# Which engine adds the residual: GpSimd for all tiles but one, VectorE keeps products and low parts

## The chip, the cores and the metric

One core of a Trainium2 chip runs the whole program. Its engines are TensorE (matrix products), VectorE, ScalarE, GpSimd and SyncE (which here only issues DMAs); they run their own instruction streams and meet at semaphores. The metric is the device time of one execution in microseconds.

## What is computed

The reference is one inference step of a decoder trunk with two layers, for 256 prompt tokens and 8 x 4 sample tokens, so 288 tokens of width 1024 in all. Layer 0 mixes tokens by dilated and sliding-window attention, layer 1 by retention; each is followed by a squared-ReLU MLP. Every one of these four sublayers stands between two norms, and what this case is about is the line that adds its result to x:

```python
def _rmsnorm(x, g):
    y = xf * lax.rsqrt(jnp.mean(xf * xf, axis=-1, keepdims=True) + NORM_EPS)
    return (y * g.astype(jnp.float32)).astype(x.dtype)

for layer in range(DEPTH):
    ...
    xp = xp + _rmsnorm(mp, gn[1])
    xs = xs + _rmsnorm(ms, gn[1])
    xp = xp + _rmsnorm(_mlp(_rmsnorm(xp, gn[2]), w_ff1[layer], w_ff2[layer]), gn[3])
    xs = xs + _rmsnorm(_mlp(_rmsnorm(xs, gn[2]), w_ff1[layer], w_ff2[layer]), gn[3])
return (xp, xs, ...)
```

## The kernel before

Activations lie transposed: `x` and `y` are tiles of 128 partitions (features) by KT = 8 tiles by T = 288 tokens, in float32. Every weight product is made of three passes: a float32 operand is split into a high part (ScalarE copies it into a rounded type: `hH` for x, `wH` for a weight strip) and a low part (VectorE takes the operand minus its high part: `hL` by `split_x`, line 1616; `wL` by `split_strip`, line 1607). A product of one feature tile with one strip is then three matmuls for each of two output halves (`tile_product`, lines 610 to 612).

Weights come in strips of 128 x 2048, loaded by SyncE, rounded by ScalarE, split by VectorE, two ahead of TensorE.

Between two sublayers lies a joint. The code numbers them e = 0 to 3: after the mixer's output product, after the first MLP, after the retention's output product, and after the second MLP, which is the end of the program. In a joint:

- ScalarE has copied the sublayer's output, scaled by the post-norm's gain, from PSUM into `y`, and squared it; TensorE sums the squares over the features, ScalarE takes the root (`token_root`), VectorE the reciprocal, and TensorE spreads the result over the partitions into the PSUM bank `MS` (`spread_root`).
- VectorE goes through groups of feature tiles, `X_GROUPS` (tile 0, tile 1, tiles 2-3, 4-5, 6-7; at the end `X_LAST`: 0-1, 2-3, 4-5, 6-7). For each: the product y = y * MS (line 1652, semaphore `t_done`), then the low parts of the group before (`split_x`), then the addition x = x + y (line 1656, semaphore `x_done`). The loop is in `residual`.
- ScalarE waits for each group's `x_done` (`pre_norm`, line 1240), rounds its tiles with the pre-norm's gain (`round_x`, line 1235) and squares them into `y` (line 1243) for the next norm.
- TensorE fills the wait with products that nobody reads (`N_RUN`, line 675) and then takes tile after tile as `hx_split` counts them (`first_strips`, line 679): for each tile ten matmuls, six for one strip and four for the next (line 690), then the rest of the second strip (line 698).
- After the last low part VectorE splits the next weight strip (line 1666) and goes on in its own `pre_norm` (lines 1625 to 1635).

At the end there is no next product: SyncE waits for the groups in order and stores each (lines 546 and 547), then waits for the stores.

GpSimd's stream is short. It zeroes some tiles, copies sample queries into place (line 563), issues stores of the caches, then waits for the last strip before the retention, zeroes `vpad` and `kpad` (lines 576 and 577), which ScalarE needs in the retention, and issues the stores of the states (lines 581 and 585). The order of each engine's work is written by hand; nothing is scheduled by a planner.

Of the kernel before, what the change touches and what calls it, by code (L numbers as in the profile page):

```python
# [17 lines left out]
ALU = mybir.AluOpType  # L18
# [5 lines left out]
KT = D // P  # L24
# [99 lines left out]

X_GROUPS = ((0, 1), (1, 1), (2, 2), (4, 2), (6, 2))
X_LAST = ((0, 2), (2, 2), (4, 2), (6, 2))

# [24 lines left out]
def build_program(nc, wst, x_in, cols, trig, mats, pmask, dmask, rmask, qkdec, kcache, vcache, state,  # L154
                  x_out, k_out, v_out, pstate_out, sstate_out):
    with ExitStack() as ctx:
# [12 lines left out]
        x = sb("x", [P, KT, T])  # L169
# [72 lines left out]
        with ExitStack() as ret:  # L242
# [32 lines left out]
            def unit(u):  # L275

                at = sslot[:, u % U_SLOTS, :] if u % U_SLOTS < 2 else raw[:, 0, :]
                return at.rearrange("p (n e) -> p n e", n=4)
# [59 lines left out]
        def own_head(g, hp, e):  # L338
# [4 lines left out]
                        "p (m k) (n t) -> p m k n t", m=2, t=NT)[:, :, hp, :, :],  # L343
                    src[:, :, :, hp // 2, :, 2 * (hp % 2) + e])

        def gain(layer, norm, k):
            c = C_GAIN + (4 * layer + norm) * KT + k
            return col[:, c:c + 1]
# [6 lines left out]
        g_dve, y_copied, g_act = map(sem, ("g_dve", "y_copied", "g_act"))  # L355
        hx_round, hx_split = map(sem, ("hx_round", "hx_split"))
        sq_sum, ms_done, rms_done, rs_done = map(sem, ("sq_sum", "ms_done", "rms_done", "rs_done"))
        t_done, x_done = map(sem, ("t_done", "x_done"))
        rope_mul, rope_out, trigR_done, kz_done, sel_done = map(
            sem, ("rope_mul", "rope_out", "trigR_done", "kz_done", "sel_done"))  # L360
        v_turned, v_tok, k_stored, v_stored = map(sem, ("v_turned", "v_tok", "k_stored", "v_stored"))
# [62 lines left out]
        def _(sp):  # L424
# [118 lines left out]
                    sp.dma_start(dec_k[:, :, :], qkdec[:, 1]).then_inc(rmask_in, 16)  # L543
            strips(S_RETOUT + N_RETOUT, N_STRIPS)
            for k, n in X_LAST:
                sp.wait_ge(x_done, 3 * KT + k + n)
                sp.dma_start(x_out[:, k:k + n, :], x[:, k:k + n, :]).then_inc(fin, 16)
            sp.wait_ge(fin, 16 * len(X_LAST))


        @block.gpsimd
        def _(pool):
            pool.wait_ge(rs_done, 1)
            pool.wait_ge(a_split, 1)
            for at in (vtok_flat[:, 0:6 * 512], qz(3, 0), qz(3, 1)):
                nc.gpsimd.memset(at, 0.0).then_inc(q_zero, 1)
            pool.wait_ge(q_zero, 3)
            for i, br in enumerate(Q_ORDER):
                pool.wait_ge(rope_out, 1 + 2 * (2 * i + 2))
                for s in range(2):  # L560
                    for h in range(4):
                        r = slice(32 * h, 32 * h + 32)
                        nc.gpsimd.tensor_copy(
                            qz(br, s)[r].rearrange("p z (n s t h) -> p z n s t h", n=NB, s=2, t=NT)[:, :, :, s, :, h],
                            qT[r, 4 * br + 2 * s:4 * br + 2 * s + 2, SEQ:T].rearrange(
                                "p z (n t) -> p z n t", t=NT)).then_inc(q_spread, 1)
            pool.wait_ge(g_dve, GBUF + USER[18] + 1)
            pool.dma_start(v_out[:, 0:8, :], vT[:, 0:8, :]).then_inc(v_stored, 16)
            pool.wait_ge(g_dve, GBUF + USER[20] + 1)
            pool.dma_start(v_out[:, 8:NVT, :], vT[:, 8:NVT, :]).then_inc(v_stored2, 16)  # L570
            pool.wait_ge(rope_out, 1 + 2 * 4 * NBR)
            pool.wait_ge(pv_done, N_PAIR + 4)
            pool.dma_start(k_out, kT[:, :, :]).then_inc(k_stored, 16)

            pool.wait_ge(strip_used, S_RETIN)
            nc.gpsimd.memset(vpad[:, :, :, :], 0.0).then_inc(r_zero, 1)
            nc.gpsimd.memset(kpad[:, :, :, :], 0.0).then_inc(r_zero, 1)
            for h in range(NHR):
                for z in range(2):
                    pool.wait_ge(r_scopied, 2 * h + z + 1)  # L580
                    pool.dma_start(pstate_out[h, z * P:(z + 1) * P, :], ps_sb[:, z, :]).then_inc(ps_stored, 16)
                for u in range(4 * h, 4 * h + 4):
                    g, z = u // 2 % 2, u % 2
                    pool.wait_ge(r_updated, 2 * (u + 1))
                    pool.dma_start(sstate_out[4 * g:4 * g + 4, h, z * P:z * P + P, :].rearrange("n p e -> p n e"),
                                   unit(u)).then_inc(s_stored[u % U_SLOTS], 16)
            pool.wait_ge(k_stored, 16)
            pool.wait_ge(v_stored, 16)
            pool.wait_ge(v_stored2, 16)
            pool.wait_ge(ps_stored, 16 * 2 * NHR)  # L590
            for j in range(U_SLOTS):
                pool.wait_ge(s_stored[j], 16 * (6 if j == 0 else 5))
# [629 lines left out]
        def _(act):  # L1222
# [14 lines left out]
            def pre_norm(b, layer, norm, s):  # L1237

                for k, n in X_GROUPS:
                    act.wait_ge(x_done, KT * (b - 1) + k + n)  # L1240
                    for i in range(k, k + n):
                        round_x(i, layer, norm)
                    nc.scalar.activation(y[:, k:k + n, :], x[:, k:k + n, :], ACT.Square).then_inc(xsq2, n)
                arrived, loads = landed(s + 2)
                act.wait_ge(arrived, 16 * loads)
                act.wait_ge(strip_used, s + 1)
                for done, c in ((half_round, slice(0, HALF_STRIP)), (h_round, slice(HALF_STRIP, KT * SC))):
                    nc.scalar.activation(wH[:, s % 2, c], raw[:, raw_slot(s + 2), c], ACT.Copy).then_inc(done, 1)
                round_strip(s + 3, s + 3)
                root(2 * b)  # L1250
# [353 lines left out]
        def _(dve):  # L1604
# [36 lines left out]
            def residual(e, s=None, b=None, nlayer=0, nnorm=0):  # L1641


                dve.wait_ge(rms_done, 2 * e + 2)
                nc.vector.reciprocal(tok[:, 3:6], tok[:, 0:3]).then_inc(rs_done, 1)
                dve.wait_ge(rs_spread, e + 1)
                groups = X_LAST if b is None else X_GROUPS
                behind = ()
                for k, n in groups:
                    c = slice(k, k + n)  # L1650
                    rs = MS.unsqueeze(1).broadcast_to([P, n, T])
                    nc.vector.tensor_tensor(y[:, c, :], y[:, c, :], rs, ALU.mult).then_inc(t_done, n)  # L1652
                    for i in behind:
                        split_x(b, i, nlayer, nnorm)
                    dve.wait_ge(t_done, KT * e + k + n)
                    nc.vector.tensor_tensor(x[:, c, :], x[:, c, :], y[:, c, :], ALU.add).then_inc(x_done, n)  # L1656
                    behind = range(k, k + n) if b is not None else ()
                for i in behind:
                    split_x(b, i, nlayer, nnorm)
                if b is None:  # L1660
                    return

                at = (s + SPL) % SPL
                dve.wait_ge(h_round, s + SPL + 1)
                for c, done in ((slice(0, HALF_STRIP), low_split), (slice(HALF_STRIP, KT * SC), l_split)):
                    nc.vector.tensor_tensor(wL[:, at, c], raw[:, raw_slot(s + SPL), c], wH[:, at, c].bitcast(F32),
                                            ALU.subtract).then_inc(done, 1)
# [648 lines left out]
```

## Time and profile before

| | |
|---|---|
| Time, median of 3 runs | 994.88 us (994.68 to 995.05) |
| Time of the profiled execution | 994.74 us |
| Its span, first to last instruction | 992.8 us |
| TensorE products, weight loads | 98%, 90% of the span |
| VectorE, ScalarE, GpSimd | 60%, 44%, 4% |
| Granted clock of TensorE | 0.996 |

The page gives each engine's busy share; below it, the timelines give the instructions in order of time, with what ended the idle time before them. A product of TensorE is shown with a duration of about 0.3 us, but the next one starts 0.13 us later, because they overlap; what counts is the distance of the starts. VectorE's instructions overlap too, by some 0.07 us. Spans on GpSimd are rough.

### The profile page before, as it was taken

The page shows a single profiled execution, that of the slowest core. Times are in us where ns is not written, and L with a number is a line of the kernel's source. Part 1 is how long each engine was busy: PE and PEld are TensorE (multiplying, and loading weights), DVE is VectorE, ACT ScalarE, POOL GpSimd, SP SyncE. Part 2 cuts the span into 40 slices and gives each one's busy share as a digit, 9 for nine tenths or more (in the row PEclk, how much of TensorE's full clock was granted, in tenths as well). Part 3 has the DMA queues.
Part 4 walks back from the last instruction along what each step waited for, and adds up shares of the span by engine and source line. Part 5 has one row for each costly group of instructions (what it writes and reads, how often), then busy time and mean ns, then how long its engine had stood idle before and what let it go on. Part 6 is the DMA issues. An engine that isn't in the chain of part 4 may idle for free. (4 is left out here: it accounts for less than half of the span.)

```text
span 992.8 us, 17813 instructions
## 1 busy us (share of the span) xinstructions
PE 971.7 (98%) x7580; PEld 894.5 (90%) x7580; DVE 595.6 (60%) x769; ACT 432.0 (44%) x544; POOL 35.5 (4%) x68
## 2 busy tenths in 40 slices
PE   8999999999999999999999999999999999999996
PEld 8988998657999999999988878788799999999996
DVE  6756654666686553334875767675683775553343
ACT  5231224676655443333542534435344554443331
POOL 0310000000000000000001010100100000000000
PEclk9999999999999999999999999999999999999998
DMA  9887759856344444443556858685764254444421
GB/s 353 332 288 264 271 198 349 313 187 250 127 170 171 169 169 166 159 164 146 205 182 243 323 186 303 222 291 196 272 248 170 86 209 164 162 161 160 166 79 48
DMA packets 50702, 206.63 MB, mean 208 GB/s; under 512 B 3536, under 2 KB 3920, under 8 KB 35024
## 3 DMA queue, kind: packets, MB, share of 16 engines
q1 hardware_dynamic: 45216, 182.58, 51.6%
q0 software_dynamic: 5424, 23.15, 6.2%
q8 instruction: 48, 0.79, 0.3%
q14 instruction: 14, 0.11, 0.0%
HBM read 181.39 MB, written 24.33 MB: 207 GB/s over the span
## 5 line engine op out<-in xcount | busy, mean ns | idle before, releaser
L610 PE MATMUL banks<-hH,wH 128*128 128x288 f32 x1248 | 375.7, 301 | 4.3 <-DVE hL L1616 2.8
L1229 ACT ACTIVATE wH<-raw 128x2048 fp32r<-128x2048 f32 x116 | 222.3, 1916 | 360.9 <-PE banks L612 358.3
L1607 DVE TENSOR_TENSOR wL<-raw,wH 128x2048 fp32r<-128x2048 f32 x113 | 258.8, 2290 | 188.3 <-ACT wH L1229 188.0
L612 PE MATMUL banks<-hH,wL 128*128 128x288 f32 x1248 | 368.6, 295 | 0.0
L611 PE MATMUL banks<-hL,wH 128*128 128x288 f32 x1248 | 368.5, 295 | 0.0
L610 PEld LDWEIGHTS banks<-hH,wH 128*128 128x128 f32 x1248 | 236.4, 189 | 19.8 <-issue 10.2
L611 PEld LDWEIGHTS banks<-hL,wH 128*128 128x128 f32 x1248 | 235.6, 189 | 0.4
L612 PEld LDWEIGHTS banks<-hH,wL 128*128 128x128 f32 x1248 | 235.1, 188 | 0.0
L612 PE MATMUL banks<-aH,wL 128*128 128x288 f32 x512 | 151.8, 296 | 0.0
L610 PE MATMUL banks<-aH,wH 128*128 128x288 f32 x512 | 151.3, 296 | 0.0
L611 PE MATMUL banks<-aL,wH 128*128 128x288 f32 x512 | 149.3, 292 | 0.0
L611 PEld LDWEIGHTS banks<-aL,wH 128*128 128x128 f32 x512 | 97.6, 191 | 0.0
L610 PEld LDWEIGHTS banks<-aH,wH 128*128 128x128 f32 x512 | 96.2, 188 | 0.0
L612 PEld LDWEIGHTS banks<-aH,wL 128*128 128x128 f32 x512 | 95.9, 187 | 0.0
L2021 DVE SCALAR_TENSOR_TENSOR sslot<-sslot,banks 128x1024 f32<-128x1024 f32 x22 | 26.8, 1220 | 28.7 <-PE banks L1117 28.7
L1710 DVE SCALAR_TENSOR_TENSOR relu_sb<-banks,norms 128x576 f32<-128x576 f32 x32 | 24.0, 756 | 31.5 <-PE banks L612 31.5
L610 PE MATMUL banks<-yH,wH 128*128 128x288 f32 x128 | 38.3, 300 | 0.0
L612 PE MATMUL banks<-yH,wL 128*128 128x288 f32 x128 | 37.9, 296 | 0.0
L611 PE MATMUL banks<-yL,wH 128*128 128x288 f32 x128 | 37.3, 292 | 0.0
L1691 DVE TENSOR_TENSOR sqacc<-banks,trigs 128x576 f32<-128x576 f32 x24 | 18.2, 757 | 29.2 <-PE banks L612 28.9
L1715 DVE TENSOR_TENSOR aL<-a_sb,aH 128x576 f32 (+1 forms) x32 | 24.1, 752 | 4.8 <-ACT aH L1311 4.8
L1309 ACT ACTIVATE a_sb<-relu_sb 128x576 f32<-128x576 f32 x32 | 21.4, 670 | 7.2 <-DVE aL L1715 7.2
(292 smaller groups left out, 996.4 us busy)
## 6 DMA issues: line engine op xcount, KB each, us to landing
raw<-wst SPq DMA_DIRECT2D x120, 1024.0 KB, 4.9
cache_sb<-kcache SPq DMA_DIRECT2D x14, 1024.0 KB, 7.6
sslot<-state SPq DMA_DIRECT2D x11, 1024.0 KB, 7.8
sstate_out<-sslot POOLq DMA_DIRECT2D x11, 1024.0 KB, 6.8
raw<-vcache SPq DMA_DIRECT2D x6, 1024.0 KB, 10.1
w_area<-vcache SPq DMA_DIRECT2D x6, 1024.0 KB, 13.0
raw<-state SPq DMA_DIRECT2D x5, 1024.0 KB, 8.4
sstate_out<-raw POOLq DMA_DIRECT2D x5, 1024.0 KB, 5.5
```

Source lines behind the costliest of these rows:

```text
L610: nc.tensor.matmul(out[:, m, :], wH[:, u % 2, c], hi[:, k, :], start=first, stop=False)
L611: nc.tensor.matmul(out[:, m, :], wH[:, u % 2, c], lo[:, k, :], start=False, stop=False)
L612: return nc.tensor.matmul(out[:, m, :], wL[:, u % 2, c], hi[:, k, :], start=False, stop=last)
L1229: nc.scalar.activation(wH[:, at % SPL, :], raw[:, raw_slot(at), :], ACT.Copy).then_inc(h_round, 1)
L1309: nc.scalar.activation(a_sb[:, :, :], relu_sb[:, u % 2, :, :], ACT.Square).then_inc(relu_sq, 1)
L1607: nc.vector.tensor_tensor(wL[:, at % SPL, :], raw[:, raw_slot(at), :], wH[:, at % SPL, :].bitcast(F32), ALU.subtract).then_inc(l_split, 1)
L1691: nc.vector.tensor_tensor(sq[:, :, :], src, both(trigR[:, 0, :]), ALU.mult).then_inc(rope_mul, 1)
L1710: nc.vector.scalar_tensor_tensor(out=relu_sb[:, u % 2, :, :], in0=out, scalar=0.0, in1=both(rs_pre[:, :]), op0=ALU.max, op1=ALU.mult).then ...
L1715: nc.vector.tensor_tensor(aL[:, ds(8 * i + 2 * u, 2), :], a_sb[:, :, :], aH[:, ds(8 * i + 2 * u, 2), :].bitcast(F32), ALU.subtract).then_i ...
L2021: nc.vector.scalar_tensor_tensor(out=c, in0=c, scalar=GAMMA[u // 4] ** NT, in1=banks[:, 6:8, :], op0=ALU.mult, op1=ALU.add).then_inc(r_upd ...
```

## The change

A second semaphore, `x_added`, counts the additions that GpSimd makes. VectorE keeps the addition of one group: tile 0 in the three joints (`X_OWN`), tiles 6-7 at the end (`X_OWN_LAST`). All others go to GpSimd (`add_x`), which waits for the product's `t_done` and adds a group at a time. Those who need a group (ScalarE in the joints, SyncE at the end) wait for `x_done` or `x_added`, as `x_ready` says. In GpSimd's stream the additions of joints 0 and 1 stand before the zeroing of `vpad` and `kpad`, those of joint 2 and of the end behind the stores of the states. VectorE's products and low parts keep their order.

```diff
--- before.py
+++ after.py
@@ -126,6 +126,9 @@
 X_LAST = ((0, 2), (2, 2), (4, 2), (6, 2))
+X_OWN, X_OWN_LAST = (0, 1), (6, 2)
 N_RUN = (5, 14)
@@ -343,6 +346,16 @@
                         "p (m k) (n t) -> p m k n t", m=2, t=NT)[:, :, hp, :, :],
                     src[:, :, :, hp // 2, :, 2 * (hp % 2) + e])
+        def on_pool(e):
+            return [g for g in X_GROUPS if g != X_OWN] if e < 3 else [g for g in X_LAST if g != X_OWN_LAST]
+        def x_ready(e, k, n):
+            if (k, n) == (X_OWN if e < 3 else X_OWN_LAST):
+                return x_done, e + 1
+            return x_added, (KT - 1) * e + k + n - (1 if e < 3 else 0)
         def gain(layer, norm, k):
             c = C_GAIN + (4 * layer + norm) * KT + k
             return col[:, c:c + 1]
@@ -355,7 +368,7 @@
         g_dve, y_copied, g_act = map(sem, ("g_dve", "y_copied", "g_act"))
         hx_round, hx_split = map(sem, ("hx_round", "hx_split"))
         sq_sum, ms_done, rms_done, rs_done = map(sem, ("sq_sum", "ms_done", "rms_done", "rs_done"))
-        t_done, x_done = map(sem, ("t_done", "x_done"))
+        t_done, x_done, x_added = map(sem, ("t_done", "x_done", "x_added"))
         rope_mul, rope_out, trigR_done, kz_done, sel_done = map(
             sem, ("rope_mul", "rope_out", "trigR_done", "kz_done", "sel_done"))
         v_turned, v_tok, k_stored, v_stored = map(sem, ("v_turned", "v_tok", "k_stored", "v_stored"))
@@ -543,13 +556,19 @@
                     sp.dma_start(dec_k[:, :, :], qkdec[:, 1]).then_inc(rmask_in, 16)
             strips(S_RETOUT + N_RETOUT, N_STRIPS)
             for k, n in X_LAST:
-                sp.wait_ge(x_done, 3 * KT + k + n)
+                sp.wait_ge(*x_ready(3, k, n))
                 sp.dma_start(x_out[:, k:k + n, :], x[:, k:k + n, :]).then_inc(fin, 16)
             sp.wait_ge(fin, 16 * len(X_LAST))
         @block.gpsimd
         def _(pool):
+            def add_x(e):
+                for k, n in on_pool(e):
+                    pool.wait_ge(t_done, KT * e + k + n)
+                    nc.gpsimd.tensor_tensor(x[:, k:k + n, :], x[:, k:k + n, :], y[:, k:k + n, :], ALU.add).then_inc(x_added, n)
             pool.wait_ge(rs_done, 1)
             pool.wait_ge(a_split, 1)
             for at in (vtok_flat[:, 0:6 * 512], qz(3, 0), qz(3, 1)):
@@ -571,7 +590,8 @@
             pool.wait_ge(rope_out, 1 + 2 * 4 * NBR)
             pool.wait_ge(pv_done, N_PAIR + 4)
             pool.dma_start(k_out, kT[:, :, :]).then_inc(k_stored, 16)
-
+            add_x(0)
+            add_x(1)
             pool.wait_ge(strip_used, S_RETIN)
             nc.gpsimd.memset(vpad[:, :, :, :], 0.0).then_inc(r_zero, 1)
             nc.gpsimd.memset(kpad[:, :, :, :], 0.0).then_inc(r_zero, 1)
@@ -584,6 +604,8 @@
                     pool.wait_ge(r_updated, 2 * (u + 1))
                     pool.dma_start(sstate_out[4 * g:4 * g + 4, h, z * P:z * P + P, :].rearrange("n p e -> p n e"),
                                    unit(u)).then_inc(s_stored[u % U_SLOTS], 16)
+            add_x(2)
+            add_x(3)
             pool.wait_ge(k_stored, 16)
             pool.wait_ge(v_stored, 16)
             pool.wait_ge(v_stored2, 16)
@@ -1237,7 +1259,7 @@
             def pre_norm(b, layer, norm, s):
                 for k, n in X_GROUPS:
-                    act.wait_ge(x_done, KT * (b - 1) + k + n)
+                    act.wait_ge(*x_ready(b - 1, k, n))
                     for i in range(k, k + n):
                         round_x(i, layer, norm)
                     nc.scalar.activation(y[:, k:k + n, :], x[:, k:k + n, :], ACT.Square).then_inc(xsq2, n)
@@ -1652,8 +1674,9 @@
                     nc.vector.tensor_tensor(y[:, c, :], y[:, c, :], rs, ALU.mult).then_inc(t_done, n)
                     for i in behind:
                         split_x(b, i, nlayer, nnorm)
-                    dve.wait_ge(t_done, KT * e + k + n)
-                    nc.vector.tensor_tensor(x[:, c, :], x[:, c, :], y[:, c, :], ALU.add).then_inc(x_done, n)
+                    if (k, n) == (X_OWN if b is not None else X_OWN_LAST):
+                        dve.wait_ge(t_done, KT * e + k + n)
+                        nc.vector.tensor_tensor(x[:, c, :], x[:, c, :], y[:, c, :], ALU.add).then_inc(x_done, 1)
                     behind = range(k, k + n) if b is not None else ()
                 for i in behind:
                     split_x(b, i, nlayer, nnorm)
```

## Rows read from the trace of the kernel before

**Rows 1.** The page's engine table, busy us, share of the span, instructions.

```profile
PE 971.7 (98%) x7580; PEld 894.5 (90%) x7580; DVE 595.6 (60%) x769; ACT 432.0 (44%) x544; POOL 35.5 (4%) x68
```

**Rows 2.** Timeline, third joint, VectorE: start us, us, line, operation, output<-inputs, [idle <-releaser].

```profile
774.81 0.45 DVE L1652 TENSOR_TENSOR y<-y,banks 128x288 f32<-128x288 f32 x1 [0.70 <-PE banks L666]
775.30 0.46 DVE L1656 TENSOR_TENSOR x<-x,y 128x288 f32<-128x288 f32 x1
775.67 0.45 DVE L1652 TENSOR_TENSOR y<-y,banks 128x288 f32<-128x288 f32 x1
776.36 0.52 DVE L1616 SCALAR_TENSOR_TENSOR hL<-x,col,hH 128x288 fp32r<-128x288 f32 x1 [0.24 <-ACT hH L1235]
776.80 0.45 DVE L1656 TENSOR_TENSOR x<-x,y 128x288 f32<-128x288 f32 x1
777.16 0.75 DVE L1652 TENSOR_TENSOR y<-y,banks 128x576 f32<-128x576 f32 x1
777.85 0.52 DVE L1616 SCALAR_TENSOR_TENSOR hL<-x,col,hH 128x288 fp32r<-128x288 f32 x1
778.29 0.75 DVE L1656 TENSOR_TENSOR x<-x,y 128x576 f32<-128x576 f32 x1
...
779.65 0.95 DVE L1616 SCALAR_TENSOR_TENSOR hL<-x,col,hH 128x288 fp32r<-128x288 f32 x2
```

**Rows 3.** The same timeline, ScalarE, rounding of tile 0.

```profile
775.79 0.54 ACT L1235 ACTIVATE hH<-x,col 128x288 fp32r<-128x288 f32 x1
```

**Rows 4.** The same timeline, TensorE: first products of tiles 0, 2, 3 and 4.

```profile
776.93 0.40 PE L610 MATMUL banks<-hH,wH 128*128 128x288 f32 x1 [0.31 <-DVE hL L1616]
...
780.22 0.40 PE L610 MATMUL banks<-hH,wH 128*128 128x288 f32 x1 [0.20 <-DVE hL L1616]
...
781.65 0.29 PE L610 MATMUL banks<-hH,wH 128*128 128x288 f32 x1
...
782.97 0.30 PE L610 MATMUL banks<-hH,wH 128*128 128x288 f32 x1
```

**Rows 5.** Timeline, end of the program, VectorE and the last issue of SyncE.

```profile
984.14 0.75 DVE L1652 TENSOR_TENSOR y<-y,banks 128x576 f32<-128x576 f32 x1 [0.77 <-PE banks L666]
...
985.00 0.76 DVE L1656 TENSOR_TENSOR x<-x,y 128x576 f32<-128x576 f32 x1
...
989.58 0.76 DVE L1656 TENSOR_TENSOR x<-x,y 128x576 f32<-128x576 f32 x1
...
990.37 0.33 SPq L547 DMA_DIRECT2D x_out<-x  x1
```

**Rows 6.** Groups of instructions on GpSimd: operation, shapes xcount | busy us, mean ns | idle.

```profile
L577 POOL MEMSET kpad<- 128x512 f32 x1 | 0.5, 524 | 0.0
...
L2296 POOL MEMSET const-float32-0.0<- 128x1 f32 x1 | 0.1, 99 | 0.3 <-issue 0.3
```

**Rows 7.** Timeline of GpSimd ahead of the second joint.

```profile
471.33 0.95 POOL L576 MEMSET vpad<- 128x1024 f32 x1 [235.33 <-PE banks L612]
```

**Rows 8.** Timeline of GpSimd's copies, 31 to 36 us, three of eight.

```profile
31.45 0.30 POOL L563 COPY vtok<-qT 32x64 f32<-32x64 f32 x1 [4.13 <-DVE qT L1698]
...
32.89 2.30 POOL L563 COPY vtok<-qT 32x64 f32<-32x64 f32 x1
...
35.25 0.35 POOL L563 COPY vtok<-qT 32x64 f32<-32x64 f32 x1
```

**Rows 9.** Timeline of VectorE, the same stretch.

```profile
31.41 0.76 DVE L1691 TENSOR_TENSOR sqacc<-banks,trigs 128x576 f32<-128x576 f32 x1
...
32.75 2.28 DVE L1607 TENSOR_TENSOR wL<-raw,wH 128x2048 fp32r<-128x2048 f32 x1
...
34.95 0.49 DVE L1697 TENSOR_TENSOR qT<-sqacc 128x288 f32<-128x288 f32 x1
```

**Rows 10.** TensorE's timeline near 506; windows (PE, PEld, DVE, ACT, POOL busy, clock, DMA).

```profile
506.72 0.55 PE L1017 MATMUL banks<-mat,vTr 128*128 128x128 f32 x3 [1.04 <-DVE vTr L2111]
...
505.00:506.70 1.70, 0.68 (x6) 0.44 (x4) 1.63 (x4) 0.32 (x1) 0.00 (x0) 1.00 1.11 445
```

## The prediction

> **What bounds the kernel now.** I read the page's engine table first [rows 1]: TensorE is busy 971.7 us of a span of 992.8 us. So time can come or go only where TensorE waits, and after its last product. There are three joints (after the mixer's output projection, after the first MLP, after the retention's output projection) where one sublayer's result becomes the next one's input, and the end of the program. They look alike; I work out the third.
>
> In the VectorE timeline [rows 2] the reader is to see an alternation: product (L1652), add (L1656), low part (L1616). Times from here on are us after the first product's start, 774.81. Tile 0: product 0 to 0.45, add to 0.95; ScalarE rounds it from 0.98 to 1.52 [rows 3]; VectorE takes its low part 1.55 to 2.07; TensorE starts on it at 2.12 after 0.31 of idleness [rows 4]. Tile 1's low part starts at 3.04. Tiles 2 and 3 come out of one add (3.48 to 4.23); TensorE takes tile 2 at 5.41 with 0.20 of idleness [rows 4] and then never runs dry before tile 7, since one tile feeds it for 1.32 us (tiles 3 and 4 start at 781.65 and 782.97: ten products at 0.13 us) and VectorE makes two in 2.2 us. So of a joint only the arrivals of tiles 0, 1 and 2 set the time; faster deliveries later are worth nothing. How much is to be won at most: from TensorE's 2.12, two tiles of 1.32 end at 4.76, and tile 2 starts at 5.41, so 0.65 us per joint.
>
> At the end [rows 5] VectorE alternates four products and four adds of pairs of tiles, from 984.14 to 990.34, each pair costing about 1.53 us; the last store is issued at 990.37 and the span ends 2.4 us later. Here all of VectorE's time is on the path.
>
> The profiled execution took 994.74 us (span 992.8 plus 1.9 around it), 0.14 below the median 994.88.
>
> **The price of a GpSimd add.** No row shows a GpSimd instruction with two inputs. The nearest are memsets of 512 and 1024 columns with 0.524 and 0.95 us [rows 6, 7], which is 0.83 ns per column and 0.10 fixed, as the memset of one column also shows, and a copy of 64 columns with 0.30 [rows 8]. Lower bound: 0.10 plus two operands at 0.83 ns, 1.06 us for 576 columns and 0.58 for 288. Upper bound: the whole excess of the copy put down to its columns, (0.30-0.10)/64 = 3.1 ns each, so 1.9 us and 1.0 us. I take the copy's 0.30 as the fixed part and two operands at the memset's slope, 1.26 us and 0.78 us: the memsets are nearest in size, the copy in kind. VectorE needs 0.75 and 0.45 for the same [rows 2].
>
> The Trainium skill (GPSIMD Engine Reference, Elementwise, side-by-side cycle accounting) gives 4497 ns for a GpSimd add of 2048 columns against 2293 ns on VectorE. The trace agrees with the VectorE figure (2.28 us in [rows 9]); no row shows the other. An estimate from that page is 1.31 us for 576 columns and 0.68 for 288, and the sum below would come out the same within 0.1 us per joint.
>
> **Do the two engines hold each other up?** This decides the case. In the GpSimd timeline [rows 8] a copy that normally takes 0.30 starts at 32.89 and takes 2.30; it ends at 35.19. In the VectorE timeline [rows 9] the low part L1607, with two inputs in SBUF (raw, wH), runs from 32.75 to 35.03. The copy at 31.45 lies inside L1691, whose inputs are PSUM banks and one SBUF tile, and takes its 0.30. So a GpSimd read waits while VectorE reads two SBUF tiles, until about 0.14 before VectorE's instruction ends (35.19-0.30 = 34.89), and not while it reads PSUM and SBUF. The reverse shows weakly: the instruction at 34.95 takes 0.49 where its like takes 0.45 or 0.46 and the copy at 35.25 takes 0.35. These copies read 64 columns in 32 partitions, so they could hold VectorE for no more than this; an add of 576 columns reads some 9 times as long.
>
> The Trainium skill (SBUF — State Buffer, section "SBUF: two separate sides") says that VectorE with two SBUF inputs and GpSimd share a port pair as an exclusive lock, and that whoever starts first has it for the whole instruction. By that rule, with which the 2.30 us copy agrees, the low parts of x (x and hH, both SBUF) wait for GpSimd's adds; without it the sum would be that of the first rival.
>
> **The joint, step by step.** I let every such reader hold the other from its start to 0.14 before its end. A GpSimd start costs 0.06 after its releaser, a ScalarE one 0.03. The change removes four of five adds from VectorE (0.45 + 3 x 0.75 = 2.7 us), puts them on GpSimd, and adds a hop VectorE to GpSimd to ScalarE.
> Tile 1's product ends at 1.31; GpSimd adds 1.37 to 2.15. Tile 0's low part could start at 1.55 but is held to 2.01, and ends at 2.53: TensorE starts at 2.58, +0.46.
> Product 2-3 behind it: 2.45 to 3.20. Tile 1's low part 3.13 to 3.65, in time, since TensorE needs it at 4.0. It holds GpSimd's add of 2-3 until 3.51: 3.51 to 4.77.
> ScalarE has rounded tile 2 by 5.34, and its low part could start then, where before it starts at 4.84. But product 4-5 was done at 4.32, so GpSimd goes straight on to add 4-5, 4.77 to 6.03, holding to 5.89. The low part of tile 2 ends at 6.41, TensorE takes it at 6.46 in place of 5.41: +1.05 us. That contains the 0.46.
> After that: product 6-7 at 6.8 to 7.5, low parts of 4 and 5 done at 7.95 and (held by add 6-7 until 8.93) 9.45, needed at 9.2 and 10.5; low part 6 at about 10.2, needed at 11.8. The weight strip's low part (L1666) comes a little later and still before TensorE's next strip at 13.5 + 1.05. So the later tiles are covered by the 1.32 us that each feeds TensorE. ScalarE's next strip waits for TensorE and shifts with it. Three joints: +3.15 us.
>
> **The end.** Products now run back to back, every 0.69 us, ending at 0.75, 1.44, 2.13 and 2.82 (after 984.14). GpSimd: 0-1 from 0.81 to 2.07, 2-3 to 3.33. VectorE's own add of 6-7 (two SBUF inputs) would start at 2.93, is held to 3.19 and ends at 3.95; add 4-5 is held by it to 3.81 and ends at 5.07. SyncE issues in the order of pairs, so the store of 6-7 goes behind that of 4-5: 5.10, and 0.35 later 5.45, where the last issue now stands at 6.23 [rows 5]. Gain 0.78 us.
>
> **What is queued behind the new waits.** GpSimd now stands in the adds of the first two joints before it zeroes vpad and kpad (L576, L577); they ran at 471.33 [rows 7], just ahead of the second joint, and come some 15 us later; ScalarE first needs them near 507, so some 20 us of cover are left, and without it each us would be one at the head of the retention. Stores on GpSimd's queue ahead of each joint have been issued long before, and its closing waits on stores come after all. SyncE waits for another semaphore, no more. ScalarE's wait at the head of each group changes its source only.
>
> **Sum.** +3.15 - 0.78 = +2.4 on 994.74, 997.1 profiled, 997.3 as a median.
>
> **The rivals.**
> (1) VectorE is not held: only GpSimd waits, or neither. For it: the delay of VectorE in [rows 9] is only 0.03 us. Against: the 0.35 of the next copy, so that both sides gave way. Tile 0 then stays at 2.12, tile 1 arrives 0.17 earlier, product 2-3 ends at 2.73, add 2-3 at 4.05 (4.38 if the low part goes first), TensorE takes tile 2 at 5.21 to 5.54: -0.2 to +0.1 per joint. The end: adds to 4.59, last issue 4.97, -1.26. Total -1.9 to -0.9, so 993.1. This is the side of faster, and it decides if the low parts that lie inside a GpSimd add keep their 0.52 us.
> (2) Cheap GpSimd add, 1.06 and 0.58 us: the same steps give tile 2 at 5.86, +0.45 per joint, and -1.24 at the end: +0.1, 995.0.
> (3) Dear GpSimd add, 1.9 and 1.0 us: tile 2 at 7.96, +2.55 per joint, and +1.1 at the end: +8.8, 1003.7. The break-even lies near 1.05 us per add of 576 columns.
> (4) TensorE's longer idleness (1.1 us ahead of tile 2) costs its clock. Against: 1.04 us of idleness at 506.72 with a granted clock of 1.00, the upper level of 2.4 GHz, in the stretch [rows 10]. At 1.2 GHz each product would take twice 0.13 us: 1.3 us per tile, so several us, about 1002.
> That the change does not do what it says I leave at nearly nothing: GpSimd has no other work at any joint. A first use that loads code would cost once: the first copy, at 31.45, took 0.30 like the later ones [rows 8]. The Trainium skill (GPSIMD Engine Reference, Instruction dispatch) has about 6 us for the first call of a freshly loaded kernel; no run here shows that, and by it the time would be near 1003.
>
> **How the numbers follow.** Forecast 0.58, rival (1) 0.15, (2) 0.15, (3) 0.08, (4) with a load 0.04. A measurement of this kernel can tell some 0.2%, 2.0 us, from no change; the forecast's +2.4 lies just beyond, so I count two thirds of it as slower. Slower 0.38+0.08+0.04 = 0.50; same 0.20+0.15+0.05 = 0.40; faster 0.10, all from (1). The likeliest one's own range is 995.5 to 1000. For 8 in 10 the range goes from 993.5, in the middle of (1)'s values, to 1001, short of (3).
>
> **What would show it.** Right: the low part of tile 0 starts at the end of GpSimd's first add, TensorE idles about 0.8 us before tile 0 and 1.1 us before tile 2, GpSimd's adds last about 1.3 us, the last store is issued about 5.5 us after the first product. Wrong: low parts of 0.52 us that lie inside GpSimd adds; adds far from 1.26 us; TensorE running dry at tiles 4 to 7 instead; a granted clock under 1.00 in a joint.

## The result, and the profile after

The changed kernel takes 998.88 us (median of 7 runs, 998.35 to 998.98) against 995.05 for the kernel before in the same comparison (994.68 to 996.39): ratio 1.0036, interval 1.0025 to 1.0047. It is slower by 3.8 us. The forecast was slower by 2.4, at 997.3.

A joint can be measured without its surroundings: the distance from its first product (the first L1652 of the joint before, L1674 after) to the next joint's first product, or to the end of the span. Four sections, in us:

| section | before | after | difference |
|---|---|---|---|
| joint 1 and the first MLP | 209.28 | 210.50 | +1.22 |
| joint 2 and the retention | 301.01 | 302.24 | +1.23 |
| joint 3 and the second MLP | 209.33 | 210.57 | +1.24 |
| the end | 8.66 | 8.82 | +0.16 |

With -0.15 ahead of the first joint this is the 3.7 us by which the spans differ. Where a section is left as it was, its length comes back within 0.1 us in every profile, so these four numbers, not the whole time, are what I read the experiments from (an experiment whose number of runs isn't given ran once): the stretch ahead of the first joint alone moves by up to 1.0 us from profile to profile (it ends at 264.11 to 265.12).

First the changed kernel's page, engine table. Against [rows 1] the reader is to see GpSimd's busy time grow from 35.5 to 56.0 us, while TensorE's doesn't (971.7 before, 969.5 now): the longer span is idleness.

```profile
PE 969.5 (97%) x7580; PEld 892.8 (90%) x7580; DVE 593.4 (60%) x754; ACT 431.6 (43%) x544; POOL 56.0 (6%) x83
```

The third joint of the changed kernel, VectorE and then GpSimd (start us, us, engine, line, operation, output<-inputs, and what ended idle time). The first product stands at 777.11; subtract it to compare with [rows 2].

```profile
777.11 0.45 DVE L1674 TENSOR_TENSOR y<-y,banks 128x288 f32<-128x288 f32 x1 [0.70 <-PE banks L688]
777.98 0.45 DVE L1674 TENSOR_TENSOR y<-y,banks 128x288 f32<-128x288 f32 x1
778.66 0.95 DVE L1638 SCALAR_TENSOR_TENSOR hL<-x,col,hH 128x288 fp32r<-128x288 f32 x1 [0.24 <-ACT hH L1257]
779.54 0.74 DVE L1674 TENSOR_TENSOR y<-y,banks 128x576 f32<-128x576 f32 x1
780.20 0.51 DVE L1638 SCALAR_TENSOR_TENSOR hL<-x,col,hH 128x288 fp32r<-128x288 f32 x1
780.63 0.74 DVE L1674 TENSOR_TENSOR y<-y,banks 128x576 f32<-128x576 f32 x1
782.61 1.08 DVE L1638 SCALAR_TENSOR_TENSOR hL<-x,col,hH 128x288 fp32r<-128x288 f32 x1 [1.23 <-ACT hH L1257]
...
784.71 2.11 DVE L1638 SCALAR_TENSOR_TENSOR hL<-x,col,hH 128x288 fp32r<-128x288 f32 x2
778.51 0.79 POOL L570 TENSOR_TENSOR x<-x,y 128x288 f32<-128x288 f32 x1 [51.82 <-DVE y L1674]
780.42 1.58 POOL L570 TENSOR_TENSOR x<-x,y 128x576 f32<-128x576 f32 x1 [1.12 <-DVE y L1674]
784.93 1.57 POOL L570 TENSOR_TENSOR x<-x,y 128x576 f32<-128x576 f32 x1 [1.56 <-DVE y L1674]
```

The profile shows a held instruction as a longer one, not as a later one. Tile 0's low part (778.66) takes 0.95 us in place of 0.52 [rows 2]: it lies beside GpSimd's add at 778.51 to 779.30. Tile 1's (780.20) takes 0.51: no add lies before it, and instead the add of 2-3, which starts at 780.42, takes 1.58. Tile 2's (782.61) takes 1.08: the add of 4-5 has begun by then and runs to about 783.37. The pair at 784.71 takes 2.11 in place of 0.95. TensorE in the same joint, to be laid beside [rows 4]:

```profile
779.67 0.40 PE L632 MATMUL banks<-hH,wH 128*128 128x288 f32 x1 [0.76 <-DVE hL L1638]
...
783.75 0.40 PE L632 MATMUL banks<-hH,wH 128*128 128x288 f32 x1 [1.15 <-DVE hL L1638]
```

It starts tile 0 at 2.56 us after the first product in place of 2.12, and tile 2 at 6.64 in place of 5.41, with 1.15 us of idleness ahead of it in place of 0.20. From there to the rest of the second strip (the first L698 before, L720 after) both kernels take 8.04 and 8.03 us, so nothing more is lost.

The end, VectorE, GpSimd and SyncE, beside [rows 5]:

```profile
987.68 0.76 DVE L1674 TENSOR_TENSOR y<-y,banks 128x576 f32<-128x576 f32 x1 [0.77 <-PE banks L688]
...
990.47 1.50 DVE L1679 TENSOR_TENSOR x<-x,y 128x576 f32<-128x576 f32 x1
988.58 1.41 POOL L570 TENSOR_TENSOR x<-x,y 128x576 f32<-128x576 f32 x1 [202.08 <-DVE y L1674]
989.94 1.41 POOL L570 TENSOR_TENSOR x<-x,y 128x576 f32<-128x576 f32 x1
991.30 1.92 POOL L570 TENSOR_TENSOR x<-x,y 128x576 f32<-128x576 f32 x1
993.24 0.33 SPq L560 DMA_DIRECT2D x_out<-x  x1
993.62 0.43 SPq L560 DMA_DIRECT2D x_out<-x  x1
```

GpSimd's first add lies beside products only, its second began before VectorE's add; both take 1.41 us. VectorE's own add (990.47) takes 1.50 in place of 0.76, held by GpSimd's second; GpSimd's third takes 1.92, held by VectorE's. The loss of 0.16 us is small but stands clear: the end took 8.65 to 8.75 us in the five profiles that leave it as before, and 8.78 to 8.82 in the four that have it changed.

### The profile page after: what moved, and what is told of

Read it like the earlier page. It is cut to its first block and busy times, and to the rows that moved or that the text cites. A ratio compares the mean times of both kernels' runs of the same rounds, so it can differ in the third digit from the quotient of the medians.

```text
span 996.5 us, 17814 instructions
## 1 busy us (share of the span) xinstructions
PE 969.5 (97%) x7580; PEld 892.8 (90%) x7580; DVE 593.4 (60%) x754; ACT 431.6 (43%) x544; POOL 56.0 (6%) x83
## 5 line engine op out<-in xcount | busy, mean ns | idle before, releaser
L570 POOL TENSOR_TENSOR x<-x,y 128x576 f32<-128x576 f32 (+1 forms) x15 | 20.6, 1385 | 494.4 <-DVE y L1674 494.4
```

What stands on the lines that cost most here:

```text
L570: nc.gpsimd.tensor_tensor(x[:, k:k + n, :], x[:, k:k + n, :], y[:, k:k + n, :], ALU.add).then_inc(x_added, n)
```

## The experiments

Two explanations stood against each other. The hold: a GpSimd instruction that reads SBUF and a VectorE instruction with two SBUF inputs exclude each other. The hop: GpSimd's add is merely slower (1.41 us against 0.75) and one engine further away. In every experiment the section lengths are given in the order joint 1, 2, 3, end.

### GpSimd's adds beside an unchanged joint

The kernel before; VectorE makes all its adds, and GpSimd adds a scratch tile to itself at the times of the changed kernel.

```diff
+            def beside(e):
+                for k, n in X_GROUPS[1:]:
+                    pool.wait_ge(t_done, KT * e + k + n)
+                    pool.wait_ge(x_added, (KT - 1) * e + k - 1)
+                    nc.gpsimd.tensor_tensor(tmp[:, 0:n, :], tmp[:, 0:n, :], tmp[:, 0:n, :], ALU.add).then_inc(x_added, n)
```

> The kernel before, with VectorE doing all its additions, and beside them GpSimd adds a scratch tile (tmp) to itself at the moments at which it adds in the changed kernel (after the products of tile 1, 2-3, 4-5 and 6-7 of each joint). Nobody waits for these adds. Theory of the hold (a GpSimd instruction that reads SBUF and a VectorE instruction with two SBUF inputs exclude each other): the low part of tile 0 ends some 0.45 us later, and VectorE's own add of 2-3 is held by GpSimd's of 2-3 (1.41 us), so TensorE takes tile 2 at 7.1 to 8.3 us after the first product in place of 5.41: each joint +1.7 to +2.9 us, the whole 1000 to 1003.5. Rival, the hop alone (the changed kernel is slower because GpSimd adds take 1.41 us where VectorE's take 0.75, and nobody is held): no change, 994.9 within 0.5.

Measured: 1001.83 us against 995.55 for the kernel before; sections 211.48, 303.22, 211.51, 8.72, so +2.2 us per joint. Nobody in a joint waits for these adds, so the hop is not in it at all. (One wait for them stands in the retention, before VectorE uses the scratch tile again at 510.25; the last of them was over at 487.08. The memset variant below has the same wait, and its second section is that of before.) The third joint, first product at 779.57:

```profile
781.12 0.82 DVE L1624 SCALAR_TENSOR_TENSOR hL<-x,col,hH 128x288 fp32r<-128x288 f32 x1 [0.24 <-ACT hH L1243]
...
783.35 1.70 DVE L1664 TENSOR_TENSOR x<-x,y 128x576 f32<-128x576 f32 x1
780.97 0.66 POOL L557 TENSOR_TENSOR tmp<-tmp 128x288 f32<-128x288 f32 x1 [51.83 <-DVE y L1660]
...
783.11 1.33 POOL L557 TENSOR_TENSOR tmp<-tmp 128x576 f32<-128x576 f32 x1 [1.48 <-DVE y L1660]
...
786.23 0.40 PE L618 MATMUL banks<-hH,wH 128*128 128x288 f32 x1 [1.14 <-DVE hL L1624]
```

The low part of tile 0 takes 0.82, and VectorE's own add of 2-3 (783.35) takes 1.70 in place of 0.75: it waits for GpSimd's scratch add, which ends at 784.44. The hold exists in the direction from GpSimd to VectorE, and costs more than the change did, since here VectorE's adds wait too. TensorE took tile 2 at 6.66 us, earlier than the 7.1 to 8.3 that I had expected, because VectorE's low part of tile 2 went in front of GpSimd's next scratch add. The joint lost more than tile 2's 1.25 us all the same, because TensorE ran dry again before tile 4, which it took at 9.78 in place of 8.16, and once more before tile 6.

### GpSimd writes without reading

```diff
-                    nc.gpsimd.tensor_tensor(tmp[:, 0:n, :], tmp[:, 0:n, :], tmp[:, 0:n, :], ALU.add).then_inc(x_added, n)
+                    for i in range(3):
+                        pool.wait_ge(x_added, 3 * ((KT - 1) * e + k - 1) + i * n)
+                        nc.gpsimd.memset(tmp[:, 0:n, :], 0.0).then_inc(x_added, n)
```

> As the kernel with the added scratch adds, but GpSimd fills the same moments with three memsets of tmp each (about 0.35 us for 288 and 0.58 us for 576 columns), which write SBUF and read nothing. If only reading holds VectorE: 994.9 within 0.5, low parts of 0.52 us. If any GpSimd work on SBUF holds it: at least +1.5 us per joint, 999.5 or more.

Measured: 994.85 us; sections 209.23, 301.01, 209.33, 8.75, as before within 0.1. GpSimd was busy for most of the joint and VectorE did not notice:

```profile
776.29 1.13 POOL L558 MEMSET tmp<- 128x288 f32 x3 [51.80 <-DVE y L1661]
778.13 6.22 POOL L558 MEMSET tmp<- 128x576 f32 x9 [0.71 <-DVE y L1661]
776.48 0.52 DVE L1625 SCALAR_TENSOR_TENSOR hL<-x,col,hH 128x288 fp32r<-128x288 f32 x1 [0.24 <-ACT hH L1244]
...
778.40 0.75 DVE L1665 TENSOR_TENSOR x<-x,y 128x576 f32<-128x576 f32 x1
...
779.76 0.95 DVE L1625 SCALAR_TENSOR_TENSOR hL<-x,col,hH 128x288 fp32r<-128x288 f32 x2
```

The low part of tile 0 lies inside three memsets (776.29 to 777.42) and takes 0.52; nine more fill 6.22 us, and beside them the add of 2-3 takes 0.75 and the pair of low parts 0.95, each as in [rows 2]. So GpSimd holds VectorE when it reads SBUF, not by its work as such.

### The hop kept, the hold taken away

The low part of x in the joints reads a PSUM bank in place of x, so that its value is left out of the result. Once in the changed kernel, once in the kernel before as its reference.

```diff
-in0=x[:, k, :], scalar=gain(layer, norm, k),
+in0=MS if b else x[:, k, :], scalar=gain(layer, norm, k),
```

> The changed kernel, but in the joints the low part of x reads the PSUM bank MS in place of x, so it has one SBUF input (hH) of its size; the low part's value is thereby left out of the result. The hop from VectorE to GpSimd to ScalarE and the 1.41 us adds stay. Theory of the hold: low parts do not wait, TensorE takes tile 0 at 2.12 us after the first product and tile 2 at about 5.3 (product 2-3 done at 2.73, add 2.79 to 4.20, rounded by 4.77, low part to 5.3), so the joints cost what they cost before (within 0.15 each) and only the end's +0.16 stays: 994.6 to 995.3. Rival, the hop alone: joints as in the changed kernel, +1.2 each, 998.5.

> The kernel before with the same edit of the low parts (they read the PSUM bank MS in place of x; their value is left out of the result): the reference for the kernel above. Both theories: 994.9 within 0.4, since nothing on GpSimd runs in the joints and the instruction's length is the same within 0.05 us.

Measured: 995.72 us with the change and 995.37 without it, 995.55 for the kernel before. Sections with the change 209.33, 301.08, 209.41, 8.80; without it 209.24, 300.98, 209.29, 8.67. Both times lie above what I had worked out, by 0.4 and 0.1 us; the stretch ahead of the first joint was the longest of all profiles here (265.08 and 265.12), so the two are to be compared with each other. Of the 1.2 us per joint 0.1 is left, although GpSimd still adds everything but tile 0. The changed kernel's joint so treated, first product at 775.49:

```profile
777.05 0.52 DVE L1638 SCALAR_TENSOR_TENSOR hL<-banks,col,hH 128x288 fp32r<-128x288 f32 x1 [0.24 <-ACT hH L1257]
778.29 0.52 DVE L1638 SCALAR_TENSOR_TENSOR hL<-banks,col,hH 128x288 fp32r<-128x288 f32 x1
...
780.42 0.94 DVE L1638 SCALAR_TENSOR_TENSOR hL<-banks,col,hH 128x288 fp32r<-128x288 f32 x2 [0.94 <-ACT hH L1257]
776.89 0.80 POOL L570 TENSOR_TENSOR x<-x,y 128x288 f32<-128x288 f32 x1 [51.83 <-DVE y L1674]
778.37 2.82 POOL L570 TENSOR_TENSOR x<-x,y 128x576 f32<-128x576 f32 x2 [0.68 <-DVE y L1674]
780.99 0.40 PE L632 MATMUL banks<-hH,wH 128*128 128x288 f32 x1 [0.44 <-DVE hL L1638]
```

The low part of tile 0 lies inside GpSimd's add again (777.05 within 776.89 to 777.69) and takes its 0.52, since one of its inputs is now in PSUM. TensorE takes tile 2 at 5.50, where 5.3 was worked out and 6.64 measured in the changed kernel. The hop alone costs 0.1 us per joint; the other 1.1 are the hold.

### Only the end on GpSimd

```diff
-            return [g for g in X_GROUPS if g != X_OWN] if e < 3 else [g for g in X_LAST if g != X_OWN_LAST]
+            return [] if e < 3 else [g for g in X_LAST if g != X_OWN_LAST]
```

> Joints as in the kernel before, the end as in the changed kernel (GpSimd adds pairs 0-1, 2-3 and 4-5, VectorE adds 6-7). By the two traces the end alone went from 8.66 us (first product to the end of the span) to 8.82: 995.0 to 995.1 against 994.9 before, and the rest, 3.6 us, is the joints'. If the end's loss hung on the joints, or the joints' on the end, it would be off by 0.5 us or more.

Measured: 994.82 against 994.89; sections 209.24, 300.94, 209.33, 8.82. The end is that of the changed kernel to 0.01 us, the joints are those of before. The whole time lies 0.2 under what I expected, which is the scatter of the stretch ahead of the first joint. The parts add up: the change is three joints and an end that do not touch each other.

### GpSimd for the last four tiles only

```diff
+            return [g for g in X_GROUPS if g[0] >= 4] if e < 3 else []
```

> GpSimd adds only tiles 4-5 and 6-7 of each joint, VectorE tiles 0, 1 and 2-3; the end as before. Step under test: only the arrivals of tiles 0, 1 and 2 set a joint's time, the later ones have cover. GpSimd's add of 4-5 (from about 5.0 us after the first product) may still hold the low part of tile 3, not that of tile 2, which starts at 4.84 before it: TensorE takes tile 2 at 5.4 as before, each joint within 0.3 us of before, the whole 994.5 to 995.8. If what costs is GpSimd's adds as such, wherever they lie, it is half of the change's cost: +1.8, 996.7.

Measured: 995.67 against 994.89; sections 209.60, 301.34, 209.64, 8.65: +0.3 per joint. TensorE takes tile 2 at 5.41, as expected, but tile 3 late. VectorE's low parts of 2 and 3 and the add that lies beside them:

```profile
780.15 2.11 DVE L1640 SCALAR_TENSOR_TENSOR hL<-x,col,hH 128x288 fp32r<-128x288 f32 x2
780.36 1.59 POOL L572 TENSOR_TENSOR x<-x,y 128x576 f32<-128x576 f32 x1 [55.48 <-DVE y L1676]
782.32 0.40 PE L634 MATMUL banks<-hH,wH 128*128 128x288 f32 x1
```

The pair takes 2.11 in place of 0.95. Tile 2's low part was already reading when GpSimd's add came; tile 3's was held to the end of it, and TensorE started tile 3 (782.32) at 7.01 us after the first product (775.31) in place of 6.84, and tile 4 at 8.44 in place of 8.16: 0.17 us of waiting, and 0.11 because the second product after a stop starts 0.24 after the first and not 0.13. A loss of 0.3 is neither zero, as the step in the prediction would have it, nor half of the change's cost; it stands at the edge of the 0.3 that I had allowed for tile 3.

### Tile 0's low part ahead of GpSimd's first add

```diff
                     pool.wait_ge(t_done, KT * e + k + n)
+                    if e < 3 and k == 1:
+                        pool.wait_ge(hx_split, KT * (e + 1) + 1)
```

> The changed kernel, with one wait more: GpSimd's first add of each joint waits for the low part of tile 0, so that this low part goes ahead of it. Theory of the hold: tile 0 reaches TensorE at 2.12 us again (it was 2.56), its low part takes 0.52; add of tile 1 from 2.13 to 2.9, add of 2-3 straight behind to 4.3, which now holds tile 1's low part: TensorE takes tile 1 near 4.8 and tile 2 near 6.2 in place of 6.64. Each joint -0.4 us against the changed kernel, 997.3. Rival, the hop alone: everything behind tile 0 is later by the 0.75 us that the first add starts later, each joint +0.3 to +0.7 against the changed kernel, 999.5 to 1000.5.

Measured: 997.23 against 994.89; sections 210.08, 301.83, 210.09, 8.78: against the changed kernel -0.42, -0.41, -0.48. A wait was added to the slower kernel, GpSimd's first add starts 2.22 us after the first product in place of 1.40, and the kernel got faster; by the hop alone that would have cost time. The third joint, first product at 776.33:

```profile
777.88 0.52 DVE L1640 SCALAR_TENSOR_TENSOR hL<-x,col,hH 128x288 fp32r<-128x288 f32 x1 [0.24 <-ACT hH L1259]
...
779.96 1.08 DVE L1640 SCALAR_TENSOR_TENSOR hL<-x,col,hH 128x288 fp32r<-128x288 f32 x1 [0.90 <-ACT hH L1259]
778.55 2.17 POOL L572 TENSOR_TENSOR x<-x,y 128x288 f32<-128x288 f32 x2 [52.66 <-DVE hL L1640]
781.10 0.40 PE L634 MATMUL banks<-hH,wH 128*128 128x288 f32 x1 [1.04 <-DVE hL L1640]
```

Tile 0's low part (777.88) takes 0.52 again, and tile 1's (779.96) takes 1.08 in its place, behind the add of 2-3 (the second of the two adds in 778.55 to 780.72): TensorE takes tile 1 at 4.77 after 1.04 us of idleness. That second add starts near 3.0, from the end of the row and its 1.41 us, and not at 3.31 as in the changed kernel, since product 2-3 no longer stands behind a held low part. The hold is not removed, only moved to where it costs less.

### A better end, and better joints

If only VectorE instructions with two SBUF inputs are held, GpSimd may add while VectorE makes products, which read PSUM. At the end all four products go first; GpSimd adds pair 0-1 under them, VectorE the other three pairs.

```diff
+                    for k, n in X_LAST[1:]:
+                        c = slice(k, k + n)
+                        dve.wait_ge(t_done, KT * e + k + n)
+                        nc.vector.tensor_tensor(x[:, c, :], x[:, c, :], y[:, c, :], ALU.add).then_inc(x_done, n)
...
+            pool.wait_ge(t_done, 3 * KT + 2)
+            nc.gpsimd.tensor_tensor(x[:, 0:2, :], x[:, 0:2, :], y[:, 0:2, :], ALU.add).then_inc(x_added, 2)
```

> Joints as before. At the end VectorE makes all four products first and then adds 2-3, 4-5 and 6-7; GpSimd adds only 0-1, from 0.9 to 2.3 us after the first product, while VectorE's products read PSUM and one SBUF tile. Theory of the hold: no overlap of two readers of SBUF, VectorE's adds run 2.93 to 5.1, the last store is issued at 5.1 in place of 6.23 us: 8.66 us become 7.55, the whole 993.8. If products were held too (any VectorE instruction), the first product pairs would take 1.4 us in place of 0.75 and the end would be near 8.6, no gain.

A single run gave 993.23 against 994.89; sections 209.28, 300.96, 209.32, 7.43.

```profile
983.67 2.75 DVE L1657 TENSOR_TENSOR y<-y,banks 128x576 f32<-128x576 f32 x4 [0.77 <-PE banks L671]
986.34 2.08 DVE L1671 TENSOR_TENSOR x<-x,y 128x576 f32<-128x576 f32 x3
984.58 1.40 POOL L591 TENSOR_TENSOR x<-x,y 128x576 f32<-128x576 f32 x1 [260.66 <-DVE y L1657]
988.45 0.33 SPq L550 DMA_DIRECT2D x_out<-x  x1
```

GpSimd's add takes its 1.40 us and ends at 985.98, before VectorE's adds; the four products beside it take 2.75 us, and the three adds 2.08 (0.75 for one alone, starts 0.67 apart), so none is held. The last store is issued 4.78 us after the first product in place of 6.23. How much of this is GpSimd's and how much comes of VectorE making all products first was not run. An estimate from these rows: with a fourth add on VectorE, 0.67 after the third, the last store would be issued near 5.45, which gives each about half. The same kernel in 11 runs:

> The same kernel as in the look before (at the end all products first, GpSimd adds pair 0-1 under them, VectorE the other three), now timed. Its end took 7.43 us in place of 8.66, the joints as before: ratio to the kernel before 0.9988, 1.2 us less. If the 1.7 us that the single look showed were all of the edit, 0.9983.

993.62 us against 995.24 (27 runs): ratio 0.9984, interval 0.9975 to 0.9993; its end took 7.41 in this profile. The sections give 1.25 us for the edit; the interval is too wide to tell that from the 1.6 of the medians.

Then the joints, without GpSimd: VectorE adds tile 1 before the low part of tile 0 and not behind it, in the 0.24 us in which it otherwise idles.

```diff
+                    if k == 1:
+                        dve.wait_ge(t_done, KT * e + k + n)
+                        nc.vector.tensor_tensor(x[:, c, :], x[:, c, :], y[:, c, :], ALU.add).then_inc(x_done, n)
                     for i in behind:
                         split_x(b, i, nlayer, nnorm)
+                    if k != 1:
```

> The kernel with the better end, and in each joint VectorE adds tile 1 before the low part of tile 0 in place of behind it (it idles 0.24 us there anyway); no GpSimd in the joints. Worked out as in the steps of the prediction: TensorE takes tile 0 at 2.34 in place of 2.12, product 2-3 and add 2-3 come 0.2 earlier, tile 2 at 5.2 in place of 5.41: each joint -0.2, 992.6 to 993.4, ratio 0.9982. Rival, tile 0's arrival sets a joint: each joint +0.2, and 994.3.

Measured: 992.84 us (11 runs), ratio to the kernel before 0.9977, interval 0.9968 to 0.9986; sections 209.03, 300.79, 209.11, 7.46, so -0.2 per joint as expected. Third joint, first product at 774.43:

```profile
775.78 0.46 DVE L1662 TENSOR_TENSOR x<-x,y 128x288 f32<-128x288 f32 x1
776.16 0.51 DVE L1621 SCALAR_TENSOR_TENSOR hL<-x,col,hH 128x288 fp32r<-128x288 f32 x1
...
777.68 0.76 DVE L1668 TENSOR_TENSOR x<-x,y 128x576 f32<-128x576 f32 x1
...
779.04 0.95 DVE L1621 SCALAR_TENSOR_TENSOR hL<-x,col,hH 128x288 fp32r<-128x288 f32 x2
```

Tile 0's low part starts at 1.73 in place of 1.55, the add of 2-3 at 3.25 in place of 3.48, the low part of tile 2 at 4.61 in place of 4.84. TensorE takes tile 0 at 2.30 after 0.48 us of idleness and tile 2 at 5.19, both near what was worked out; the view shows no idleness before tile 2, where it was 0.20.

Last, the add of 2-3 as two adds of one tile:

> As the kernel with tile 1's add ahead, and the addition of 2-3 is made as two additions of one tile, so that ScalarE can round tile 2 some 0.3 us earlier. Low part of tile 2 then waits for product 4-5, which VectorE has taken up before: tile 2 at TensorE near 5.1 to 5.25, each joint -0.2 to -0.3 against before, 992.4 to 993.2, ratio 0.9980. Rival: the extra instruction's 0.1 us of start-up makes later tiles late, and it is no better than the kernel with tile 1's add ahead.

Measured: 993.22 us, ratio 0.9980, interval 0.9971 to 0.9989; sections 209.06, 300.99, 209.13, 7.49. The joints are as with the single reordering or, in the second, 0.2 us worse, so its rival's outcome came true: nothing is gained. In the third joint the two adds take 0.82 us in place of 0.76, the low part of tile 2 still stands behind product 4-5, at 4.64 in place of 4.61, and TensorE takes tile 2 at 5.21. Why the second section is longer stays open. The kernel with tile 1's add ahead is the best of all that ran, 2.4 us under the kernel before and 6.0 under the changed one; its lead of 0.8 over the better end alone comes with overlapping intervals, and rests on the sections.

## Why the prediction was right, and where it was off

**That the engines hold each other up**, on which the case was put: right. It stood on one copy of 2.30 us and on 0.03 us in the other direction; the scratch adds, the memsets, and the low parts from PSUM showed it in both directions and for reads only. The exclusive lock that the Trainium skill states (SBUF — State Buffer, "SBUF: two separate sides") is what the runs show: of two such instructions the one that starts second waits and the first loses nothing (GpSimd's add of one tile took 0.79 us while it held VectorE, and 0.80 beside a low part from PSUM), and memsets, which do not read, hold no VectorE instruction with two SBUF inputs. It is let go some 0.2 us before the end that the profile shows for a GpSimd add (low part 0: 778.66+0.95-0.52 = 779.09, add to 779.30); the prediction had 0.14. Rival (1), VectorE not held, would have had 0.52 us where 0.95 was measured; it falls.

**Tile 0**: +0.46 forecast, +0.44 measured (2.56 against 2.12). The GpSimd add of one tile was put at 0.78 and took 0.79.

**Tile 2**: at 6.46 forecast, 6.64 measured, so +1.23 per joint in place of +1.05, together 0.5 us. The term that was mis-sized is the add of two tiles, 1.26 us by the copy's 0.30 plus two operands at the memset's slope. It took 1.41 alone, start to start 1.36. Two of them lie behind one another before tile 2's low part, 2.77 us in place of 2.52, of which the earlier letting go takes 0.06 back. The slope between one tile and two is (1.41-0.79)/288 = 2.2 ns per column, where twice the memset's is 1.66. The Trainium skill (GPSIMD Engine Reference, "Elementwise — side-by-side cycle accounting") has 2.6 cycles per element, and an estimate by that is 2.17 ns at its clock of 1.2 GHz; the trace agrees. The times that the prediction estimated from that page, 1.31 and 0.68 us, are 0.1 under the measured ones.

**The later tiles covered**: right for the changed kernel, whose strip ends as much later as its tile 2. As a rule it was too broad. The run with GpSimd on the last four tiles lost 0.3 us per joint by tile 3, of which my steps said only that it follows tile 2. What kept the step true in the changed kernel is that the add of 4-5 held tile 2's low part and was over when tile 3's began: the two together took 1.51 us, of which tile 2's own row has 1.08, so tile 3's was not held. The 0.65 us that was to be won at most is a little too much for the same reason as in that run: a tile taken up after a stop feeds TensorE for 1.43 us (776.93 and 777.17 are its first two products), not for 1.32.

**The end**: -0.78 forecast, +0.16 measured, the largest miss, and of the wrong sign. The order of events was right, VectorE's add held by GpSimd's second, GpSimd's third held by VectorE's. Three terms were off. The adds: the first starts at 0.90 in place of 0.81 (GpSimd started 0.08 us after a product of one tile and 0.14 to 0.15 after one of two, where 0.06 was put), and with 1.41 in place of 1.26 the last one ends 5.54 after the first product in place of 5.07, 0.47. The stores: SyncE takes 0.38 from the start of one issue to the next where I had 0.35, 0.03. And I took the time from the last issue to the end of the span as the 2.4 us of before; it was 2.9, 0.45 more. The last two stores were then issued 0.38 us apart and no longer 1.5; where they were 0.66 apart, in the better end with one pair on GpSimd, it was 2.65. No run changes only that distance, so the cause is likely, not shown. Together 0.95, the miss of 0.94 within rounding.

**The queue behind GpSimd's waits**: the memsets of vpad and kpad came at 484.21 in place of 471.33, and ScalarE first wrote those tiles at 509.18, so nobody waited for them; joint 2 with the retention lost what the two others lost. **The first use**: GpSimd's first add of the program, at 265.77, took 0.79 us like the later ones, so none was paid. **The clock**: 1.00 in all three joints in spite of 1.15 us of idleness, so rival (4) did not occur; the third:

```profile
780.00:790.00 10.00, 8.85 (x67) 8.61 (x66) 8.48 (x12) 4.71 (x10) 4.52 (x3) 1.00 0.01 2
```

**The sum**: +3.15-0.78 = +2.4 forecast, +3.69-0.15+0.16 = +3.7 measured in the spans. Both misses, 0.54 in the joints and 0.94 at the end, went the same way, so nothing cancelled: the mechanism of the joints and its size were right within about a sixth, while at the end only the order of events was. Slower by more than 0.2% had half the chance, and the range held.

## What to carry to other kernels

Before work goes to GpSimd, ask of each VectorE instruction that would run beside it how many SBUF inputs it has. Beside products that read PSUM an add of 576 columns cost 1.41 us and nobody anything; beside instructions with two SBUF inputs it delayed them nearly to its own end, and 2.7 us less work for VectorE in a joint turned into 1.2 us more in its length. In a chain of small steps look for the one tile whose arrival ends the consumer's wait, and move only what lies ahead of it: VectorE's add of tile 1, moved into 0.24 us of idleness, gave 0.2 us per joint.

## What the runs showed that I had not expected

GpSimd's add of one scratch tile to itself took 0.66 and 1.33 us, its add of x and y 0.79 and 1.41, with the same shapes. No run tells why. And a wait put in front of the slower engine, so that the other goes first, won 0.4 us per joint.
